# Feed-forward input projection: the second pair of tiles in 5 of 11 iterations by Strassen's method, weight sums by VectorE an iteration ahead, accumulators of the depthwise convolution in PSUM

## The reference

```
def conv_ffn(x, w_up, b_up, w_dw, b_dw, w_down, b_down):
    h = x @ w_up + b_up                      # 1024 -> 2 * 2816
    h = causal_depthwise_conv(h, w_dw, b_dw) # width 3
    g, val = jnp.split(h, 2, axis=-1)
    return (jax.nn.silu(g) * val) @ w_down + b_down
...
    x = layer_norm(DEEPNORM_ALPHA * x + y, norm2_g[i], norm2_b[i])
```

## Time and profile before

| | |
|---|---|
| time, median of 3 runs | 1031.15 us (1029.99 to 1031.49) |
| profiled execution, first to last instruction | 1027.8 us |
| TensorE busy | 1016.9 us (99%) |
| VectorE busy | 806.6 us (78%) |
| ScalarE busy | 504.1 us (49%) |
| GpSimd busy | 224.6 us (22%) |
| mean granted TensorE clock | 0.998 |

### The profile page before, as it was taken

The page is one execution under the profiler, slowest core; times in us unless marked ns, Lnnn a source line. Parts: engine busy times, 40 slices in busy tenths (PEclk is TensorE's granted clock), DMA queues, the critical chain, the costliest instruction groups (busy, mean ns, idle before and its releaser), DMA issues.

```text
span 1027.8 us, 14241 instructions
## 1 busy us (share of the span) xinstructions
PE 1016.9 (99%) x4731; PEld 842.4 (82%) x4731; DVE 806.6 (78%) x1156; ACT 504.1 (49%) x739; POOL 224.6 (22%) x279
## 2 busy tenths in 40 slices
PE   9999999999999999999999999999999999999997
PEld 7777787988888888888888888898888888888885
DVE  6999978687767767787895869768777776778888
ACT  6889864333334334465454443344343343346553
POOL 1998730413440000000010200052334000000001
PEclk9999999999999999999999999999999999999999
DMA  9756269899995232376655333879999523228652
GB/s 335 217 159 164 62 151 347 177 265 290 228 259 143 102 102 82 118 271 204 195 175 201 118 111 112 308 154 284 270 235 248 148 82 105 99 88 264 201 197 111
DMA packets 64428, 189.71 MB, mean 185 GB/s; under 512 B 7424, under 2 KB 8448, under 8 KB 63872
## 3 DMA queue, kind: packets, MB, share of 16 engines
q1 hardware_dynamic: 44144, 137.76, 39.4%
q0 software_dynamic: 18224, 44.05, 21.7%
q10 hardware_dynamic: 2016, 7.34, 2.0%
HBM read 178.11 MB, written 54.53 MB: 226 GB/s over the span
## 4 chain that ended last, share of the span: by engine, by line
PE 84%; DVE 3%; issue 1%; DMA 1%; ACT 1%; POOL 0%; DVEq 0%; POOLq 0%; ACTq 0%
PE ps L1671 17%; PE ps L1669 17%; PE ps L1670 17%; PE ps L1908 6%; PE ps L1907 6%; PE ps L1906 6%; PE ps L1679 4%; PE ps L1681 4%; PE ps L1680 4%; PE ps L1836 1%; DMA raw<-d_weights 1%; DVE ps L1173 1%; PE ps L1951 1%; PE ps L1953 1%; PE ps L1952 1%
## 5 line engine op out<-in xcount | busy, mean ns | idle before, releaser
L1669 PE MATMUL ps<-xh,wh 128*128 128x512 f32 x816 | 320.3, 392 | 0.4 <-DVE wl L1077 0.3
L1671 PE MATMUL ps<-xh,wl 128*128 128x512 f32 x816 | 317.6, 389 | 0.0
L1670 PE MATMUL ps<-xl,wh 128*128 128x512 f32 x816 | 317.5, 389 | 0.0
L1669 PEld LDWEIGHTS ps<-xh,wh 128*128 128x128 f32 x816 | 153.2, 188 | 33.6 <-issue 1.2
L1670 PEld LDWEIGHTS ps<-xl,wh 128*128 128x128 f32 x816 | 153.2, 188 | 32.8 <-issue 1.2
L1671 PEld LDWEIGHTS ps<-xh,wl 128*128 128x128 f32 x816 | 153.2, 188 | 32.1
L687 ACT ACTIVATE wh<-raw 128x1024 fp32r<-128x1024 f32 x114 | 119.9, 1056 | 81.4 <-PE ps L1908 63.3
L1077 DVE TENSOR_TENSOR wl<-raw,wh 128x1024 fp32r<-128x1024 f32 x101 | 122.6, 1220 | 41.7 <-ACT wh L687 39.9
L536 POOL TENSOR_SCALAR veps<-sqs 128x1 f32<-128x1 f32 x15 | 4.8, 323 | 561.5 <-ACT squares L881 561.5
L1402 DVE TENSOR_TENSOR wl<-raw,wh 128x1024 fp32r<-128x1024 f32 x80 | 97.6, 1220 | 7.6 <-ACT wh L935 7.6
L1906 PE MATMUL ps<-wh,parts 128*128 128x512 f32 x264 | 102.7, 389 | 0.0
(11 more groups left out here) (199 smaller groups left out, 1657.7 us busy)
## 6 DMA issues: line engine op xcount, KB each, us to landing
raw<-d_weights SPq DMA_DIRECT2D x156, 512.0 KB, 4.0
raw<-summed SPq DMA_DIRECT2D x56, 512.0 KB, 4.1
summed<-d_weights POOLq DMA_DIRECT2D x88, 256.0 KB, 8.1
summed<-d_weights SPq DMA_DIRECT2D x66, 256.0 KB, 7.5
summed<-summed POOLq DMA_DIRECT2D x46, 256.0 KB, 5.0
wl<-raw POOLq DMA_DIRECT2D x4, 1024.0 KB, 7.2
wl<-raw POOLq DMA_DIRECT2D x5, 512.0 KB, 7.3
xraw<-d_x_fm SPq DMA_DIRECT2D x8, 256.0 KB, 6.1
```

What stands on the lines that cost most here:

```text
L1669: eng.matmul(ps[:, bank, cols], a, xh[:, k, cols], start=(k == 0), stop=False)
L1670: eng.matmul(ps[:, bank, cols], a, xl[:, k, cols], start=False, stop=False)
L1671: mm = eng.matmul(ps[:, bank, cols], b, xh[:, k, cols], start=False, stop=(k == KD - 1))
```

## The change

In iterations 2 to 6 of both layers (`S_FROM`, `S_TO`) the units c = 2 and c = 3 are not multiplied by `up`. They are taken as a 2x2 block matrix (two tiles by two halves of the input channels), x as one too (two halves of the channels by two halves of the positions), and seven products take the place of eight. Each of the seven (`part`) is 12 matmuls of 256 columns.

- **Sums of x**: GpSimd makes four of them (`t_f`) once per layer (`x_sums`), 20 instructions of 512 elements, ahead of `summed_weights`. ScalarE and VectorE split them (`token_parts`, 4 instructions of 1024 elements each) in iteration 1. TensorE waits for the four low parts (`t_lo`) before it enters the loop of iteration 2.
- **Sums of weights**: VectorE makes four per iteration in place in `raw` (`first_sums`, `second_sums`), one iteration ahead. One half unit is split before (`second`), three sums are split after (`strassen`, first lines). SyncE loads into those two slots only when the sums have been split (`s_lo`).
- **Products kept apart**: partial results are copied out of PSUM amid the seven products (`kept`, `snap`), and VectorE adds the others (`block`, `st_rd`).
- **Taps**: in iterations 0 to 6 the accumulators of the convolution lie in PSUM. In all iterations the newest tap is made by ScalarE from the bank (`started`; two ScalarE instructions per tile in place of one), and VectorE has two taps instead of three.
- **Hidden parts** of iterations 2 to 6 are split in one go after iteration 7 (instructions of 1280 elements).
- Tiles have other places in SBUF, and iteration 1 stands outside the loop on ScalarE and VectorE.

```diff
+S_FROM, S_TO = 2, 7
...
+            if strassen_pair(u - RAW):
+                m, c = strassen_pair(u - RAW)
+                eng.wait_ge(s_lo, 3 * m + (3 if c == 2 else 1))
...
+        def x_sums(layer):
+            eng.wait_ge(x_lo, XN[2 * layer])
...
+            def both(out, a, b, op):
+                for rows in (slice(0, 2), slice(2, 4)):
+                    eng.tensor_tensor(out[:, rows, :], a[:, rows, :], b[:, rows, :], op).then_inc(t_sum, 1)
+            both(t_f[0], b12[0], b11[0], ALU.subtract)
+            both(t_part[0], b12[1], b11[1], ALU.subtract)
+            eng.wait_ge(t_sum, n + 4)
+            both(t_f[0], t_f[0], t_part[0], ALU.add)
...
+        def up_sums(layer):
+            x_sums(layer)
+            summed_weights(layer)
...
+            def started(i, q, v, accs):
+                buf, signal = pads[v]
+                bank = ps[:, bank0 + 2 * q + v, :]
+                eng.wait_ge(w_used, i * 4 + (u0 + 2 * q + v + 1))
+                eng.wait_ge(tap, i * 4 * LATER + (first_tap + 2 * LATER * q - LATER + LATER * v))
+                eng.activation(buf[:, FPAD:], bank, ACT.Identity, bias=par[:, bass.ds(column(i, q, v) + C_FUP_B, 1)])
+                if v == 0:
+                    products_read(i, q)
+                eng.activation(accs[v], bank, ACT.Identity, scale=par[:, bass.ds(newest_at(i, q, v), 1)],
+                               bias=tapb[:, bass.ds(column(i, q, v), 1)]).then_inc(signal, 1)
...
...
+            def token_parts(js):
+                for j in js:
+                    eng.wait_ge(t_sum, 2 * (T_SUMS * layer + T_ENDS[j]))
+                    eng.activation(t_h[j], t_f[j], ACT.Copy).then_inc(t_hi, 1)
+            def strassen(i, more):
+                eng.wait_ge(w_used, i * 4 + u0)
+                eng.wait_ge(s_sum, i * 4 + (4 * m0 + 2))
+                eng.activation(wh[:, three, :], raw[:, raw3, :], ACT.Copy).then_inc(s_hi, 1)
+                eng.wait_ge(s_sum, i * 4 + (4 * m0 + 3))
+                eng.activation(sum2h[:, :], raw[:, raw2, 0:HALF], ACT.Copy).then_inc(s_hi, 1)
+                eng.wait_ge(s_sum, i * 4 + (4 * m0 + 4))
+                eng.activation(sum4h, raw[:, raw2, HALF:UNIT], ACT.Copy).then_inc(s_hi, 1)
+                started(i, 0, 0, in_banks)
+                ahead(i, 1)
+                started(i, 0, 1, in_banks)
+                eng.wait_ge(st_pe, i * 5 + (5 * m0 + 1))
+                kept(i, 0, 0, x_bank)
+                gate(i, 0, in_banks)
+                ahead(i, 2)
+                eng.wait_ge(st_pe, i * 5 + (5 * m0 + 2))
+                kept(i, 1, 1, y_bank)
+                eng.wait_ge(st_pe, i * 5 + (5 * m0 + 3))
+                kept(i, 0, 1, x_bank)
+                ahead(i, 3)
+                eng.wait_ge(st_pe, i * 5 + (5 * m0 + 4))
+                kept(i, 1, 0, z_second)
+                if more:
+                    second(i + 1)
+                products_read(i, 1)
+                for v, (buf, signal) in enumerate(pads):
+                    eng.wait_ge(st_rd, i * 4 + (4 * m0 + 2 * v + 2))
+                    eng.activation(in_banks[v], buf[:, FPAD:], ACT.Identity, scale=par[:, bass.ds(newest_at(i, 1, v), 1)],
+                                   bias=par[:, bass.ds(column(i, 1, v) + C_FDW_B, 1)]).then_inc(signal, 1)
+                gate(i, 1, in_banks)
+            def first_strassen(c):
+                ahead(S_FROM - 1, c)
+                if c == 2:
+                    token_parts((0, 1))
+                if c == 3:
+                    token_parts((3, 2))
+                    eng.wait_ge(res_ok, NT * (2 * layer + 1))
+                    second(S_FROM)
...
+            def taps(i, q, v, accs):
+                buf, signal = pads[v]
+                eng.wait_ge(signal, i * 2 + (q + layer * KH + 1))
+                for k in range(1, FTAPS):
...
+                    if k > 1:
+                        eng.wait_ge(tap, i * 4 * LATER + (first_tap + 2 * LATER * q + LATER * v + k - 1))
+                    eng.scalar_tensor_tensor(out=accs[v], in0=buf[:, off:off + SEQ], scalar=par[:, bass.ds(cw, 1)],
+                                             in1=accs[v], op0=ALU.mult, op1=ALU.add).then_inc(tap, 1)
...
+            def block(i, v, t, bank):
+                part = pads[v][0][:, FPAD + t * HQ:FPAD + (t + 1) * HQ]
+                c = (i * 2 + 1) * 2 + (C_FUP_B + 2 * KH * layer + v)
+                eng.scalar_tensor_tensor(out=part, in0=bank, scalar=par[:, bass.ds(c, 1)], in1=part,
+                                         op0=ALU.add, op1=ALU.add).then_inc(st_rd, 1)
+            def second(i):
+                eng.wait_ge(w_hi, i * 4 + (u0 + 4))
+                eng.tensor_tensor(v2l[:, :], raw[:, raw3, HALF:UNIT], v2h[:, :].bitcast(f32), ALU.subtract).then_inc(w_lo, 1)
...
+            def first_sums(i):
+                eng.wait_ge(w_lo, i * 4 + (u0 + 4 - len(BY_DMA)))
+                eng.tensor_tensor(q22, q21, q22, ALU.add).then_inc(s_sum, 1)
+                eng.tensor_tensor(q21, q11, q21, ALU.subtract).then_inc(s_sum, 1)
+            def second_sums(i):
+                eng.wait_ge(s_sum, i * 4 + (4 * m0 + 2))
+                eng.tensor_tensor(q11, q22, q11, ALU.subtract).then_inc(s_sum, 1)
+                eng.wait_ge(s_sum, i * 4 + (4 * m0 + 3))
+                eng.tensor_tensor(q12, q12, q11, ALU.subtract).then_inc(s_sum, 1)
+            def token_parts(ns):
+                for n in ns:
+                    j = (0, 1, 3, 2)[n]
+                    eng.wait_ge(t_hi, 4 * layer + n + 1)
+                    eng.tensor_tensor(t_l[j], t_f[j], t_h[j].bitcast(f32), ALU.subtract).then_inc(t_lo, 1)
+            def strassen(i, more):
+                for n, (l, f, h) in enumerate(((wl[:, three, :], b, wh[:, three, :]), (sum2l[:, :], q11, sum2h[:, :]), (sum4l, q12, sum4h))):
+                    eng.wait_ge(s_hi, i * 3 + (3 * m0 + n + 1))
+                    eng.tensor_tensor(l, f, h.bitcast(f32), ALU.subtract).then_inc(s_lo, 1)
+                taps(i, 0, 0, in_banks)
+                ahead(i, 1)
+                taps(i, 0, 1, in_banks)
+                product(i, 0, in_banks)
+                ahead(i, 2)
+                eng.wait_ge(w_used, i * 4 + (u0 + 3))
+                eng.wait_ge(snap, i * 4 + (4 * m0 + 1))
+                block(i, 0, 0, z_first)
+                ahead(i, 3)
+                if more:
+                    second(i + 1)
+                eng.wait_ge(st_pe, i * 5 + (5 * m0 + 5))
+                eng.wait_ge(snap, i * 4 + (4 * m0 + 3))
+                block(i, 0, 1, y_bank)
+                if more:
+                    first_sums(i + 1)
+                eng.wait_ge(w_used, i * 4 + (u0 + 4))
+                eng.wait_ge(snap, i * 4 + (4 * m0 + 4))
+                block(i, 1, 1, x_bank)
+                block(i, 1, 0, x_bank)
+                if more:
+                    second_sums(i + 1)
+                taps(i, 1, 0, in_banks)
+                taps(i, 1, 1, in_banks)
+                product(i, 1, in_banks)
+            def first_strassen(c):
+                ahead(S_FROM - 1, c)
+                if c == 2:
+                    token_parts((0, 1))
+                if c == 3:
+                    second(S_FROM)
+                    first_sums(S_FROM)
+                    second_sums(S_FROM)
+                    token_parts((2, 3))
+            regular(0, lambda c: los([u0 + c + LEAD] if c else []), in_banks)
             residual(2 * layer + 1)
...
+            regular(S_FROM - 1, first_strassen, in_banks)
+            with eng.Fori(S_FROM, S_TO - 1) as i:
+                strassen(i, True)
+            strassen(S_TO - 1, False)
...
+            eng.wait_ge(h_hi, KH * layer + 2 * S_TO)
+            eng.tensor_tensor(n5[:, late_rows, :], a21[:, late_rows, :], a22[:, late_rows, :], ALU.subtract).then_inc(a_sum, NS)
+            for l, f, h in ((a11l, a11, a11h), (a12l, a12, a12h)):
+                eng.tensor_tensor(l[:, late_rows, :], f[:, late_rows, :], h[:, late_rows, :].bitcast(f32),
+                                  ALU.subtract).then_inc(h_lo, NS)
+            eng.wait_ge(a_sum, 2 * KQ * layer + 2 * (S_TO + 1) - NS)
+            eng.tensor_tensor(s2[:, late_rows, :], n5[:, late_rows, :], a11[:, late_rows, :], ALU.subtract).then_inc(a_sum, NS)
...
+            def part(o, w_h, w_l, x, begins):
+                for k in range(KD // 2):
...
+                    eng.matmul(o, a, x[0][:, k, :], start=(begins and k == 0), stop=False, skip_group_check=True)
+                    eng.matmul(o, a, x[1][:, k, :], start=False, stop=False, skip_group_check=True)
+                    mm = eng.matmul(o, b, x[0][:, k, :], start=False, stop=(k == KD // 2 - 1), skip_group_check=True)
+                return mm
+            def strassen_units(i):
+                eng.wait_ge(w_lo, i * 4 + (u_up + 3 - len(BY_DMA)))
+                eng.wait_ge(v_in, i * 2 + KH * layer)
+                part(x_bank, wh[:, two, first], wl[:, two, first], b11, True).then_inc(st_pe, 1)
```

(25 more changed lines are left out.)

312 lines of the change are left out of this document (209 added, 103 removed).

## The result

| | before | the change |
|---|---|---|
| time, median | 1030.57 us (1028.72 to 1031.49) | 1057.36 us (1056.89 to 1060.23) |
| profiled execution, first to last instruction | 1027.8 us | 1058.4 us |
| TensorE busy | 1016.9 us (99%) | 1018.2 us (96%) |
| mean granted TensorE clock | 0.998 | 0.982 |

The ratio is 1.0268 (1.0252 to 1.0284): slower by 26.8 us. The prediction was 1043, range 1034 to 1052. The sign and the place are as predicted; the loss is about 14 us larger than the forecast had it, and the time lies outside the range. The profiled execution was the slowest of the four of the change (1060.23 us), so the spans differ by more than the medians: by 30.6 us.

A forecast was written before the change was run, and what follows sets the result against it. TensorE, 99% busy, was taken as the bound. Span 1027.8 less 8.0 (products) plus 16.0 (stops) plus 4.0 (clock) is 1039.8; with 3.35 from profiled span to median, 1043 us, range 1034 to 1052.

The forecast's parts named there:

- The products: TensorE, iterations 2 to 6: seven narrow parts replace two units, 10.08 against 10.88 us; saves 0.80 per iteration, 8.0 in all.
- VectorE in the loop: Iterations 2 to 6: VectorE needs 18.6 us of TensorE's 20.96 per iteration, so the loop holds its 8.0 us.
- The 2 us of margin: TensorE's other waits in the loop, such as for snapshots, were each said to have 2 us or more to spare.
- rival 3: In the loop, loads of weights become the bound through the ring of load, splits, sums and product: 1047 to 1060; chance 0.14.
- The entry into iteration 2: TensorE waits for `t_lo` until VectorE's late split is done at about 237.2: 8.0 us per layer, 16.0 in all.
- rival 1: Ahead of iteration 2 the wait for `t_lo` is covered, so the change is faster: 1023 us; chance 0.09.
- The clock: Behind the stop at iteration 2 TensorE resumes at 1.2 GHz: 2.0 us lost per layer, 4.0 in all.
- What else moves: GpSimd's DMA issues come some 35 us later, behind its additions, to about 345; hidden, at no cost.

The follow-up runs named there:

- e4: The change without the sums of x (no additions, splits or wait for them; products use blocks of x itself): 1025.38 us, 0.9952 of the kernel before.
- e9: The change with TensorE's wait for `t_lo` behind the two ordinary units and three fills for each GpSimd addition: 1026.97 us, 0.9973 of the kernel before.
- e5: The change with each of GpSimd's 20 additions per layer replaced by three memsets, one after the other: 1042.81 us, 1.0128 of the kernel before.
- e8: The kernel before with 20 GpSimd additions per layer that nobody reads, placed where the change has them: 1054.84 us, 1.0239 of the kernel before.
- e1: The change with GpSimd's 20 additions per layer replaced by 20 memsets of the same tiles: 1056.66 us, 1.0265 of the kernel before.

## Why the prediction was off by 14 us

- **The products: right.** 0.80 us per iteration; measured 20.93 us per iteration against 20.96, and 84 matmuls of 256 columns 0.119 us apart.
- **VectorE in the loop: right for the change, too hopeful in itself.** No wait of TensorE from 252 to 460, and VectorE is busy for 17.6 us of an iteration (84%), where the prediction counted 18.6 and near 90%. But e4 and e9 show waits of 1 to 2 us where TensorE gives no head start. The 2 us of margin that the prediction saw everywhere hold only after a stop. That fits rival 3. The measured 1057 lies in the span of times that rival gave, 1047 to 1060, but its mechanism isn't what cost the change its time, since the loop has no wait.
- **The entry into iteration 2: right in place and cause, the term mis-sized.** Forecast 8.0 us of stop per layer; measured 11.5, and 2.85 more one unit earlier. With quiet additions it is 8.1 (e5).
- **The step that failed** is the sentence against rival 1, that VectorE's chain "is a plain sum of instructions whose durations hardly vary", and with it the treatment of GpSimd: the prediction asked whether its additions end in time (by 221 forecast, 224.2 measured) and never what they do to the engine beside them. Against e5 the change's VectorE begins the residual at 218.52, not 212.40, and needs 7.91 us for it, not 4.62: 9.4 us, which TensorE pays as 6.3 us of stop and 3.0 more at the lower clock (4.6 against 1.6), twice: 18.6 of the 18.8 us between the two spans.
- **The rows looked at had another mask, and the trace had rows without it.** GpSimd's additions of the convolution module ran beside VectorE instructions that had an operand in PSUM, and those aren't stretched. But at the end of that module the trace of the kernel before has three more additions, and beside them a VectorE instruction whose tensor operands all lie in SBUF. VectorE, then GpSimd:

```profile
132.55 1.70 DVE L1225 TENSOR_SCALAR ctm<-ctm,mv,rstd 128x256 f32<-128x256 f32 x2
136.72 0.72 DVE L1225 TENSOR_SCALAR ctm<-ctm,mv,rstd 128x256 f32<-128x256 f32 x2
131.61 2.49 POOL L568 TENSOR_TENSOR gsum<-gsum,prods 128x256 f32<-128x256 f32 x3 [1.95 <-DVE ctm L1225]
```

The same pair takes 1.70 us beside the additions and 0.72 behind them. So the effect could have been read before the run, and the prediction overlooked it. The Trainium skill has a rule for it (SBUF — State Buffer, Who interferes with whom): a VectorE instruction with two inputs in SBUF contends with a GpSimd instruction that reads SBUF, not with one that only writes it. The rows agree on both halves: beside the additions such instructions stretch, beside the fills of e5 they don't. The sentence speaks of two inputs; here instructions with one tensor input and a scalar per partition stretch as well (the pair above, and L1380 of e8, 0.54 to 1.51). The page was not weighed in the prediction, and would have been a reason for a wider range.
- **The clock: right to have a price.** 2.0 us per layer forecast; 4.6 in the trace of the change (1.7 behind the first stop, which wasn't forecast, and 2.9 behind the second), 1.6 in that of e5.
- **What else moves: right for the change.** The later DMAs of GpSimd were hidden. Had they stayed early beside the new loads, they would have cost: e1 shows landings of 18.0 us and a stop of 15.5.

## What to carry to other kernels

When work is given to an idle engine, ask of its neighbours not only whether they wait for it, but which memory its operands share with theirs: here the idle GpSimd cost 14.6 us when it added in SBUF beside VectorE. Look in the trace of before for the same instruction with and without that neighbour. Put a wait right ahead of the first instruction that needs it, and price the work that an in-order engine has up to there, since reordering that work moves the wait and doesn't shorten it. And an experiment that removes a suspect should keep the time that the suspect took, or what follows it on its engine moves too (e1).

## What the runs showed of the hardware that I had not expected

- **VectorE beside GpSimd's additions.** With all tensor operands in SBUF: 1024 elements 1.22 to 2.31 us; 256 elements 0.42 to 1.51; 512 elements times a scalar 0.54 to 1.51. At most each of these loses 1.0 to 1.1 us whatever its length, nearly one whole addition of GpSimd (1.28 alone); on average it is less (3.29 us for the four of the residual). This looks like one waiting for the other's instruction to end, as the Trainium skill has it (SBUF — State Buffer, SBUF: two separate sides: whichever of the two starts first has the shared ports for its whole instruction, and the other blocks); that the two take turns was not tested apart. With one operand in PSUM: 0.75 for a tap, unchanged. Fills: no effect (the residual of e5 took 4.62). ScalarE's copies of 1024 elements took 1.05 and 1.06 us beside the additions, as ever.
- **The lower clock lasted differently long** after the resumption: 3.4 us of the timeline in e5 after a stop of 8.1 us, 6.0 in the change after 11.5. The stop of 2.85 us was enough as well: there the first matmuls behind it still came 0.24 to 0.34 us apart, and the granted clock was 0.50 from 228.91 to 231.47.
- **Load times depend on company.** 512 KB landed in 8.2 us, and in 18.0 when GpSimd's copies of weights lay in the same stretch (e1).
